# Recurrent stage of a two-block model: gated inputs on GpSimd, the third convolution one unit later

## The chip, the cores and the metric

The program runs on one core of a Trainium2 chip. The metric is the device time of one execution in microseconds (us). The core has TensorE (PE in the profile; its weight loads are PEld), VectorE (DVE), ScalarE (ACT), GpSimd (POOL) and SyncE (SP), each with an instruction queue of its own that is worked off in order. They meet through semaphores.

## The reference, cut to what matters

The reference is two blocks of two layers each on 512 tokens of width 1024, in float32. The change touches only the recurrent mixer, which runs once, in the last layer of the second block:

```python
proj = h @ w_in                                   # 1024 -> 2048
gate, xr = jnp.split(proj, 2, axis=-1)
gate = jax.nn.gelu(gate, approximate=True)
xc = conv(xr, conv_w) + conv_b                    # causal, 4 taps, one filter per channel
r = sigmoid(einsum('bsni,nij->bsnj', xg, w_a) + b_a)   # xg is xc in 4 blocks of 256 channels
i = sigmoid(einsum('bsni,nij->bsnj', xg, w_i) + b_i)
log_a = -8 * r * softplus(-lam)
a = exp(log_a)
u = sqrt(-expm1(2 * log_a)) * (i * xc)
hs[t] = a[t] * hs[t-1] + u[t]                     # an associative scan over time
return (hs * gate) @ w_out
```

The product that changes its engine is `i * xc`.

## The kernel before

Activations lie transposed: 128 channels on the partitions, the 512 tokens along the free dimension, so a 1024-wide tensor is 8 blocks [128, 512]. A float32 matmul is made of three: weights and activations are split into a high and a low part, and hi·hi, lo·hi and hi·lo are summed in PSUM.

The input projection of the recurrent stage is 16 **units** (u0 to u15), each 8 chunks of three matmuls. Units 0 to 7 give the blocks of `xr` (tile rgx), 8 to 15 those of `gate` (rggate). For each unit the raw weights come by DMA into `wraw`, ScalarE rounds them to `whi` (L238), VectorE subtracts to get `wlo` (L245), and only then may TensorE begin the unit: it waits for `w_split`. `whi` and `wlo` have two slots. VectorE also takes every finished unit out of PSUM (L1026).

The rest of the mixer runs beside these units. Every engine walks one common list, `order`: position 8u+c stands for chunk c of unit u, and the table `beside` (L3056 to L3073) names what is to be issued behind that chunk. The steps are:

- conv (pair p, L2979): the convolution of blocks 2p and 2p+1 on VectorE, two scalings (L2982) and six multiply-adds (L2988), then the semaphore rg_xc. It stands at 19, 35, 51 and 67.
- gates (block b, L2993 and L3005): four float32 matmul instructions on TensorE (L3001, two for each of the two gates; the trace shows each as two), then on ScalarE two sigmoids into rgA and rgU (L3007, L3008) and a tanh into rgTH (L3010), which raises rg_gates. At 29, 33, 45, 49, 76, 81, 86, 91.
- input (block b, L3012): VectorE multiplies rgU by rgxc (L3014), two positions behind its gates.
- logs (block b, L3016 and L3025): ScalarE takes two logarithms and an exponential (L3020, L3021, L3023), VectorE subtracts (L3027). At 53, 57, 61, 65 for blocks 0 to 3 and at 94, 98, 102, 106 for the others.
- mult (block b, L3029 and L3033): ScalarE's last exponential (L3031), then VectorE's product rgU by rgTH (L3035) and the scan over time (L3037), two positions behind the logs.
- gelu, gated and mix close the stage. GpSimd does six of the eight gated products (L3046), its only work in this stage next to two weight DMAs.

In each unit the rounding of the next unit's weights stands at chunk 1 on ScalarE, the low part at chunk 2 on VectorE, and the previous unit's evacuation at chunk 0. So at one position VectorE meets the unit's own work first and then the entries of `beside`.

```python
if kk == 0 and u:
    evac(u - 1)
if kk == 2 and u >= 2:
    lo_part(v, 0, st, u + 1, body[u + 1] if u + 1 < nu else st["next"])
```

Of the kernel before, what the change touches and what calls it, by code (L numbers as in the profile page):

```python
# [9 lines left out]
ALU = mybir.AluOpType  # L10
# [87 lines left out]
def build_program(nc, t, out):  # L98

    with ExitStack() as ctx:  # L100
# [58 lines left out]
        def S(name):  # L159
            if name not in sems:  # L160
                sems[name] = ctx.enter_context(nc.semaphore(name))
            return sems[name]
# [2279 lines left out]
        for l in range(DEPTH):  # L2442
            full = l < DEPTH - 1
            n = TOK if full else SEQ
            v = lambda kind, l=l: (lambda b, s: scl[:, 3 * l + kind, 2 * b + s:2 * b + s + 1])
# [458 lines left out]
        def recurrent(m, last, gpost):  # L2904
# [6 lines left out]
            xr, A, U, xc, gate, TH = (here_at(n_, j) for j, n_ in enumerate(("rgx", "rgA", "rgU", "rgxc", "rggate", "rgTH")))  # L2911
            mlo, mhi = here_at("mix3lo", 0, F32R), here_at("mix3hi", 1, F32R)
            xcr, gm, p1, lns, lnd, mul, hs, gel, gp, mh, ml = (S(f"rg_{n_}") for n_ in (
                "xc", "mm", "gates", "logs", "logdiff", "mult", "hs", "gelu", "gated", "mixhi", "mixlo"))
            col = lambda name, i: VC[:, 2, B2ROW[name] + i:B2ROW[name] + i + 1]

            body, outs = [], []
# [47 lines left out]
            def dve_units(v):  # L2965
                def evac(u):
                    v.wait_ge(S("w_used"), g0 + u + 1)
                    outs[u][1](v, 0, u, unit_bank(u)).then_inc(S(f"evac_done{u % 2}"), 1)
                for u in range(nu):
                    for kk in range(8):  # L2970
# [4 lines that stand above are left out]
                        yield  # L2975
                evac(nu - 1)
                yield

            def dve_conv(v, pair):  # L2979
                for b in (2 * pair, 2 * pair + 1):  # L2980
                    v.wait_ge(*evacuated(b))
                    v.tensor_scalar(xc[:, b, :], xr[:, b, :], col("rg_conv_w", 24 + b), col("rg_conv_b", b),  # L2982
                                    ALU.mult, ALU.add)
                for j in range(3):
                    v.drain()
                    sh = 3 - j
                    for b in (2 * pair, 2 * pair + 1):
                        v.scalar_tensor_tensor(out=xc[:, b, sh:SEQ], in0=xr[:, b, 0:SEQ - sh],  # L2988
                                               scalar=col("rg_conv_w", 8 * j + b), in1=xc[:, b, sh:SEQ],
                                               op0=ALU.mult, op1=ALU.add)  # L2990
                v.drain().then_inc(xcr, 1)
# [17 lines left out]
                a.drain()  # L3009
                a.activation(TH[:, b, :], A[:, b, :], ACT.Tanh, scale=scl[:, 6, b:b + 1]).then_inc(p1, 1)  # L3010

            def dve_input(v, b):  # L3012
                v.wait_ge(p1, b + 1)
                v.tensor_tensor(U[:, b, :], U[:, b, :], xc[:, b, :], ALU.mult)  # L3014

            def act_logs(a, b):  # L3016
                if b % 4 == 0:
# [7 lines left out]
            def dve_logs(v, b):  # L3025
                v.wait_ge(lns, b + 1)
                v.tensor_tensor(TH[:, b, :], xr[:, b, :], TH[:, b, :], ALU.subtract).then_inc(lnd, 1)  # L3027
# [3 lines left out]
                a.activation(TH[:, b, :], TH[:, b, :], ACT.Exp, scale=0.5).then_inc(mul, 1)  # L3031

            def dve_scan(v, b):  # L3033
                v.wait_ge(mul, b + 1)
                v.tensor_tensor(U[:, b, :], U[:, b, :], TH[:, b, :], ALU.mult)  # L3035
                v.drain()
                v.tensor_tensor_scan(TH[:, b, :], A[:, b, :], U[:, b, :], 0.0, ALU.mult, ALU.add).then_inc(hs, 1)  # L3037
# [5 lines left out]
            def gated(e, b):  # L3043
                e.wait_ge(gel, b + 1)
                e.wait_ge(hs, b + 1)
                e.tensor_tensor(TH[:, b, :], TH[:, b, :], gate[:, b, :], ALU.mult).then_inc(gp, 1)  # L3046
# [5 lines left out]
            def dve_mixlo(v, b):  # L3052
                v.wait_ge(mh, b + 1)
                v.tensor_tensor(mlo[:, b, :], TH[:, b, :], mhi[:, b, :].bitcast(F32), ALU.subtract).then_inc(ml, 1)
# [2 lines left out]

            def put(at, *names):
                beside.setdefault(at, []).extend(names)
            for pair in range(4):  # L3060
                put(16 * pair + 19, ("conv", pair))
            for b, at in enumerate((29, 33, 45, 49, 76, 81, 86, 91)):
                put(at, ("gates", b))
                put(at + 2, ("input", b))
            for first, at in ((0, 53), (4, 94)):
                for j in range(4):
                    put(at + 4 * j, ("logs", first + j))
# [39 lines left out]
            def dve_program(v):  # L3107
                ramp.dve(v, st)
                dense = dve_units(v)
                for name, b in order:  # L3110
                    if name == "unit":
                        next(dense, None)
                    elif name == "conv":
                        dve_conv(v, b)
                    elif name == "input":
                        dve_input(v, b)
                    elif name == "logs":
                        dve_logs(v, b)
                    elif name == "mult":
                        dve_scan(v, b)  # L3120
                    elif name == "gated":
                        v.wait_ge(gp, b)
                        gated(v, b)
                    elif name == "mix":
                        dve_mixlo(v, b)

            def pool_program(pool):
                pool.wait_ge(S("phase_end"), 3 * phase_of["rg"])
                pool.dma_start(wa[:], t["rg_w_a_2"][0].rearrange("n (k p) j -> p (n k) j", p=P)).then_inc(S("rg_w"), 16)
                pool.dma_start(wi[:], t["rg_w_i_2"][0].rearrange("n (k p) j -> p (n k) j", p=P)).then_inc(S("rg_w"), 16)  # L3130
                for b in range(6):
                    gated(pool, b)
            phase_of["rg"] = len(phases)
            return mhi, mlo, dict(pool=pool_program, sp=lambda sp: sp_stage(sp, st), pe=pe_program, act=act_program,
                                  dve=dve_program), lambda k: (ml, k + 1)


# [5 lines left out]
        m, last = ffn(0, m0, last, b2("mix_post"))  # L3143

        *mixed, rg_part, rg_ready = recurrent(m, last, b2("ffn_post"))
        m1 = arena("mo1", [P, NB, SEQ], off=24 * K1)
        st, last, zero = squares_beside("b21", m1, in_arena, lambda ev: plain("wout3", t["rg_w_out_2"][0], 0, 8, SEQ,
# [116 lines left out]
```

## Time and profile before

| | |
|---|---|
| median of 3 runs | 2548.02 us (2547.56 to 2548.71) |
| the profiled execution's own time | 2550.76 us |
| its span | 2548.9 us |
| TensorE busy in the span | 94% |
| mean granted TensorE clock | 0.986 |
| recurrent units (u0 to u15) | about 1966.9 to 2098.9 us of the span |

TensorE is busy nearly all the time; a change elsewhere moves the end only where TensorE waits. In the timeline rows a number in brackets is the idle time of that engine just ahead of the row and what ended it. A matmul row's duration (0.39 us) is a pipelined one: matmuls start 0.23 us apart.

### The profile page before, as it was taken

The page shows a single profiled execution, that of the slowest core. Times are in us where ns is not written, and L with a number is a line of the kernel's source. Part 1 is how long each engine was busy: PE and PEld are TensorE (multiplying, and loading weights), DVE is VectorE, ACT ScalarE, POOL GpSimd, SP SyncE. Part 2 cuts the span into 40 slices and gives each one's busy share as a digit, 9 for nine tenths or more (in the row PEclk, how much of TensorE's full clock was granted, in tenths as well). Part 3 has the DMA queues.
Part 4 walks back from the last instruction along what each step waited for, and adds up shares of the span by engine and source line. Part 5 has one row for each costly group of instructions (what it writes and reads, how often), then busy time and mean ns, then how long its engine had stood idle before and what let it go on. Part 6 is the DMA issues. An engine that isn't in the chain of part 4 may idle for free.

```text
span 2548.9 us, 48743 instructions
## 1 busy us (share of the span) xinstructions
PE 2389.9 (94%) x20392; PEld 1885.1 (74%) x20392; DVE 1339.7 (53%) x2135; ACT 999.5 (39%) x1675; POOL 160.6 (6%) x213
## 2 busy tenths in 40 slices
PE   7999999888989999888899998999999999999999
PEld 5777777777767766787676666788887667788887
DVE  4347644556464654555567763655523664555422
ACT  3225443444343445354445554322223554322222
POOL 0000000343000000144000000000000010000000
PEclk9999999999999999999999999999999999999999
DMA  7721111000102111100131212233333222233332
GB/s 272 253 80 34 34 46 50 19 5 12 50 25 83 42 42 55 50 4 4 51 99 58 58 50 67 74 99 99 97 91 118 58 66 75 83 96 93 99 95 79
DMA packets 300551, 182.65 MB, mean 72 GB/s; under 512 B 5290, under 2 KB 284476, under 8 KB 300236
## 3 DMA queue, kind: packets, MB, share of 16 engines
q1 hardware_dynamic: 286940, 150.50, 20.2%
q10 hardware_dynamic: 12480, 25.17, 2.8%
q0 software_dynamic: 944, 4.27, 0.5%
q8 instruction: 144, 2.36, 0.4%
q14 instruction: 43, 0.35, 0.0%
HBM read 177.80 MB, written 2.12 MB: 71 GB/s over the span
## 4 chain that ended last, share of the span: by engine, by line
PE 80%; DVE 9%; ACT 5%; issue 3%; DVEq 3%; ACTq 1%; DMA 0%; SPq 0%
PE PW L323 11%; PE PW L325 11%; PE PW L324 11%; PE PW L413 6%; PE PW L414 6%; PE PW L415 6%; PE PW L1224 2%; PE PW L1267 2%; PE PW L1810 2%; PE PW L1805 1%; PE PW L1793 1%; DVE wlo L245 1%; PE PW L3001 1%; PE PW L980 1%; PE PW L598 1%
## 5 line engine op out<-in xcount | busy, mean ns | idle before, releaser
L245 DVE TENSOR_TENSOR wlo<-wraw,whi 128x1024 fp32r<-128x1024 f32 (+1 forms) x272 | 329.5, 1212 | 376.1 <-ACT whi L238 355.1
L238 ACT ACTIVATE whi<-wraw 128x1024 fp32r<-128x1024 f32 (+1 forms) x272 | 283.6, 1043 | 267.5 <-PE PW L325 256.4
L413 PE MATMUL PW<-hhi,whi 128*128 128x512 f32 (+1 forms) x880 | 323.7, 368 | 11.7 <-DVEq L3210 7.0
L323 PE MATMUL PW<-hhi,whi 128*128 128x512 f32 (+1 forms) x824 | 315.4, 383 | 0.0
L324 PE MATMUL PW<-hhi,wlo 128*128 128x512 f32 (+1 forms) x824 | 315.0, 382 | 0.0
L325 PE MATMUL PW<-hlo,whi 128*128 128x512 f32 (+1 forms) x824 | 314.9, 382 | 0.0
L414 PE MATMUL PW<-hhi,wlo 128*128 128x512 f32 (+1 forms) x880 | 306.1, 348 | 0.0
L415 PE MATMUL PW<-hlo,whi 128*128 128x512 f32 (+1 forms) x880 | 305.8, 348 | 0.0
L413 PEld LDWEIGHTS PW<-hhi,whi 128*128 128x128 f32 x880 | 167.6, 190 | 57.5 <-issue 24.0
L414 PEld LDWEIGHTS PW<-hhi,wlo 128*128 128x128 f32 x880 | 167.9, 191 | 21.8 <-issue 3.3
L415 PEld LDWEIGHTS PW<-hlo,whi 128*128 128x128 f32 x880 | 167.5, 190 | 21.7
L323 PEld LDWEIGHTS PW<-hhi,whi 128*128 128x128 f32 x824 | 155.2, 188 | 30.6 <-DVE wlo L245 0.7
L324 PEld LDWEIGHTS PW<-hhi,wlo 128*128 128x128 f32 x824 | 155.2, 188 | 30.2
L325 PEld LDWEIGHTS PW<-hlo,whi 128*128 128x128 f32 x824 | 155.1, 188 | 30.0
L323 PE MATMUL PW<-fhi,whi 128*128 128x512 f32 x352 | 138.7, 394 | 0.0
L325 PE MATMUL PW<-flo,whi 128*128 128x512 f32 x352 | 138.0, 392 | 0.0
L324 PE MATMUL PW<-fhi,wlo 128*128 128x512 f32 x352 | 136.6, 388 | 0.0
L1026 DVE TENSOR_TENSOR gb<-PW,xT 128x512 f32<-128x512 f32 x88 | 60.7, 692 | 115.3 <-PE PW L325 110.8
L1997 ACT ACTIVATE XX<-PW 128x512 f32<-128x512 f32 (+1 forms) x120 | 66.5, 554 | 118.2 <-PE PW L1810 115.3
L2860 ACT ACTIVATE gb<-gb 128x512 f32<-128x512 f32 x44 | 27.8, 632 | 210.7 <-DVE gb L1026 210.7
L1810 PE MATMUL PW<-XX,Tt 64*64 64x64 f32 x1920 | 101.6, 223 | 3.5 <-issue 2.8
L1805 PE MATMUL PW<-Tt,XX 64*64 64x64 f32 x1536 | 81.3, 233 | 16.9 <-DVE Tt L2082 12.7
(477 smaller groups left out, 4425.6 us busy)
## 6 DMA issues: line engine op xcount, KB each, us to landing
wraw<-in_w_in SPq DMA_DIRECT2D x68, 512.0 KB, 3.8
mod_w<-in_mod_w ACTq DMA_DIRECT2D x12, 2048.0 KB, 10.8
wraw<-in_ffn_w_gate SPq DMA_DIRECT2D x44, 512.0 KB, 3.8
wraw<-in_ffn_w_up SPq DMA_DIRECT2D x44, 512.0 KB, 3.8
wraw<-in_ffn_w_down SPq DMA_DIRECT2D x32, 512.0 KB, 3.8
wraw<-in_attn_w_in SPq DMA_DIRECT2D x24, 512.0 KB, 3.8
wraw<-in_w_out SPq DMA_DIRECT2D x16, 512.0 KB, 3.8
wraw<-in_rg_w_in SPq DMA_DIRECT2D x16, 512.0 KB, 4.0
```

Source lines behind the costliest of these rows:

```text
L238: act.activation(whi[:, slot, 0:kb, :], wraw[:, slot, 0:kb, :], ACT.Copy).then_inc(S("w_hi"), 1)
L245: dve.tensor_tensor(wlo[:, slot, 0:kb, :], wraw[:, slot, 0:kb, :], whi[:, slot, 0:kb, :].bitcast(F32), ALU.subtract).then_inc(S("w_split"), 1)
L323: pe.matmul(acc, wh[:, k, :], rhi[:, k0 + k, s0:s1], start=a, stop=False)
L324: pe.matmul(acc, wl[:, k, :], rhi[:, k0 + k, s0:s1], start=False, stop=False)
L325: last_mm = pe.matmul(acc, wh[:, k, :], rlo[:, k0 + k, s0:s1], start=False, stop=b)
L413: e.matmul(acc, whi[:, u % 2, k, :], rhi[:, k0 + k, s0:s1], start=k == 0, stop=False)
L414: e.matmul(acc, wlo[:, u % 2, k, :], rhi[:, k0 + k, s0:s1], start=False, stop=False)
L415: ins = e.matmul(acc, whi[:, u % 2, k, :], rlo[:, k0 + k, s0:s1], start=False, stop=k == kb - 1)
L1026: return v.tensor_tensor(self.halves(dest), self.halves(acc), self.rstd, ALU.mult)
L1805: return e.matmul(at(384 + 128 * e_ + CH * hp)[half(pi), :], XX[tp, i, 0, :], Tt[tp, i, :], start=True, stop=True)
L1810: return e.matmul(at(128 * e_ + CH * hp)[tp, :], Tt[tp, i, :], XX[tp, i, 0, :], start=True, stop=True)
L1997: a.activation(dst, src, ACT.Copy).then_inc(X_out.sem, 1)
```

## The change

GpSimd computes `i * xc` instead of VectorE, all eight blocks in a row, each when its rg_gates comes. A new semaphore, rg_entered, is raised by each product, and VectorE waits for it ahead of the product in the mult step. The convolution of pair 2 moves from position 51 (unit 6) to 59 (unit 7); the other pairs stay.

```diff
+            entered = Signal("rg_entered", 8)
...
-            def dve_input(v, b):
-                v.wait_ge(p1, b + 1)
-                v.tensor_tensor(U[:, b, :], U[:, b, :], xc[:, b, :], ALU.mult)
+            def pool_input(g, b):
+                g.wait_ge(p1, b + 1)
+                g.tensor_tensor(U[:, b, :], U[:, b, :], xc[:, b, :], ALU.mult).then_inc(entered.sem, 1)
...
             def dve_scan(v, b):
+                v.wait_ge(entered.sem, entered.at(b + 1))
                 v.wait_ge(mul, b + 1)
...
-            for pair in range(4):
-                put(16 * pair + 19, ("conv", pair))
+            for at, pair in zip((19, 35, 59, 67), range(4)):
+                put(at, ("conv", pair))
...
-                put(at + 2, ("input", b))
...
-                    elif name == "input":
-                        dve_input(v, b)
...
+                for b in range(8):
+                    pool_input(pool, b)
                 for b in range(6):
                     gated(pool, b)
```

VectorE's row before, from the low part of unit 7 to the scan of block 1. L2982 and L2988 are a convolution, L3014 an input, L3027 the logs' difference, L3035 and L3037 the product and the scan of the mult step.

```order
L245 TENSOR_TENSOR wlo<-wraw,whi 128x1024
L2982 TENSOR_SCALAR rgxc<-rgx,VC 128x512 x2
L2988 SCALAR_TENSOR_TENSOR rgxc<-rgx,VC,rgxc 128x509 x2
...
L3014 TENSOR_TENSOR rgU<-rgU,rgxc 128x512
L3027 TENSOR_TENSOR rgTH<-rgx,rgTH 128x512
L3035 TENSOR_TENSOR rgU<-rgU,rgTH 128x512
L3037 SCALAR_TENSOR_TENSOR rgTH<-rgA,rgU 128x512
L1026 TENSOR_TENSOR rgx<-PW,xT 128x512
L3027 TENSOR_TENSOR rgTH<-rgx,rgTH 128x512
L245 TENSOR_TENSOR wlo<-wraw,whi 128x1024
L3035 TENSOR_TENSOR rgU<-rgU,rgTH 128x512
L3037 SCALAR_TENSOR_TENSOR rgTH<-rgA,rgU 128x512
```

The same place now, where the lines are L3028 for the difference, L3037 and L3039 for product and scan, and L2983 and L2989 for the convolution:

```order
L245 TENSOR_TENSOR wlo<-wraw,whi 128x1024
L3028 TENSOR_TENSOR rgTH<-rgx,rgTH 128x512
L3037 TENSOR_TENSOR rgU<-rgU,rgTH 128x512
L3039 SCALAR_TENSOR_TENSOR rgTH<-rgA,rgU 128x512
L1026 TENSOR_TENSOR rgx<-PW,xT 128x512
L3028 TENSOR_TENSOR rgTH<-rgx,rgTH 128x512
L245 TENSOR_TENSOR wlo<-wraw,whi 128x1024
L2983 TENSOR_SCALAR rgxc<-rgx,VC 128x512 x2
L2989 SCALAR_TENSOR_TENSOR rgxc<-rgx,VC,rgxc 128x509 x2
...
L3037 TENSOR_TENSOR rgU<-rgU,rgTH 128x512
L3039 SCALAR_TENSOR_TENSOR rgTH<-rgA,rgU 128x512
L3028 TENSOR_TENSOR rgTH<-rgx,rgTH 128x512
```

The convolution of pair 2 has moved from ahead of the first difference to between the low part of unit 8 and the mult step of block 1; the input of block 3 is gone from the row. GpSimd's row in this stage, as a difference:

```order
-L3129 DMA rgwa<-in_rg_w_a 128x8x256
-L3130 DMA rgwi<-in_rg_w_i 128x8x256
-L3046 TENSOR_TENSOR rgTH<-rgTH,rggate 128x512 x6
+L3128 DMA rgwa<-in_rg_w_a 128x8x256
+L3129 DMA rgwi<-in_rg_w_i 128x8x256
+L3015 TENSOR_TENSOR rgU<-rgU,rgxc 128x512 x8
+L3048 TENSOR_TENSOR rgTH<-rgTH,rggate 128x512 x6
```

The eight products stand behind the weight DMAs and ahead of the gated products.

## Rows read from the trace of the kernel before

**Rows 1.** The page, first lines: busy us (share of the span) xinstructions
```profile
span 2548.9 us, 48743 instructions
PE 2389.9 (94%) x20392; PEld 1885.1 (74%) x20392; DVE 1339.7 (53%) x2135; ACT 999.5 (39%) x1675; POOL 160.6 (6%) x213
```

**Rows 2.** TensorE's waits, 1985 to 2110 us: us in total, times, longest
```profile
PE PW L2951 <- DVE wlo L245: 6.5, 4, 2.1
```

**Rows 3.** Timeline, first work of u8, u9, u10: start, us, [idle before <-releaser]
```profile
2033.87 0.50 PE L2951 MATMUL PW<-h3hi,whi 128*128 128x512 f32 x1 [2.10 <-DVE wlo L245]
...
2041.75 0.19 PEld L2951 LDWEIGHTS PW<-h3hi,whi 128*128 128x128 f32 x1 [0.96 <-DVE wlo L245]
...
2050.95 0.19 PEld L2951 LDWEIGHTS PW<-h3hi,whi 128*128 128x128 f32 x1 [0.44 <-DVE wlo L245]
```

**Rows 4.** Timeline of VectorE, from the convolution of pair 2
```profile
2020.54 1.00 DVE L2982 TENSOR_SCALAR rgxc<-rgx,VC 128x512 f32<-128x512 f32 x2
...
2026.11 0.69 DVE L3014 TENSOR_TENSOR rgU<-rgU,rgxc 128x512 f32<-128x512 f32 x1
2027.72 0.69 DVE L3027 TENSOR_TENSOR rgTH<-rgx,rgTH 128x512 f32<-128x512 f32 x1 [0.91 <-ACT rgTH L3023]
...
2031.98 0.69 DVE L3027 TENSOR_TENSOR rgTH<-rgx,rgTH 128x512 f32<-128x512 f32 x1 [0.30 <-ACT rgTH L3023]
2032.59 1.22 DVE L245 TENSOR_TENSOR wlo<-wraw,whi 128x1024 fp32r<-128x1024 f32 x1
2033.73 0.69 DVE L3035 TENSOR_TENSOR rgU<-rgU,rgTH 128x512 f32<-128x512 f32 x1
...
2035.63 0.67 DVE L3027 TENSOR_TENSOR rgTH<-rgx,rgTH 128x512 f32<-128x512 f32 x1
...
2040.48 1.22 DVE L245 TENSOR_TENSOR wlo<-wraw,whi 128x1024 fp32r<-128x1024 f32 x1
```

**Rows 5.** Timeline of ScalarE: table load behind block 3's gates; behind the difference
```profile
2024.35 1.28 ACT L3018 ACT_TABLE_LOAD   x1
...
2036.33 0.63 ACT L3031 ACTIVATE rgTH<-rgTH 128x512 f32<-128x512 f32 x1 [1.06 <-DVE rgTH L3027]
2036.87 1.04 ACT L238 ACTIVATE whi<-wraw 128x1024 fp32r<-128x1024 f32 x1
```

**Rows 6.** The chain that ended last, in order of time: start, us, what
```profile
2034.49 1.22 DVE rgTH L3037
2035.71 0.59 DVE rgTH L3027
```

**Rows 7.** By stretch: busy PE, PEld, DVE, ACT, POOL; PEclk, DMA share, GB/s
```profile
2026.20:2051.00 24.80, 22.15 (x82) 15.84 (x80) 21.15 (x27) 15.76 (x23) 0.00 (x0) 0.93 0.15 43
...
2034.70:2038.10 3.40, 3.40 (x10) 2.64 (x9) 2.63 (x4) 2.34 (x4) 0.00 (x0) 0.51 0.54 154
...
1512.40:1519.30 6.90, 5.94 (x22) 3.89 (x22) 4.75 (x11) 4.95 (x11) 0.00 (x0) 0.51 0.06 11
...
2087.40:2090.40 3.00, 2.91 (x13) 2.40 (x14) 2.23 (x4) 2.31 (x3) 0.00 (x0) 1.00 0.56 170
```

**Rows 8.** Timeline of TensorE, two other long waits
```profile
1512.35 1.22 PE L2572 MATMUL PW<-k,q 64*128 64x256 f32 x4 [3.34 <-DVEq L2723]
2087.49 0.50 PE L2951 MATMUL PW<-h3hi,whi 128*128 128x512 f32 x1 [1.95 <-DVE wlo L245]
```

**Rows 9.** Waits, 1970 to 2135 us: the inputs' (us, times, longest)
```profile
DVE rgU L3014 <- ACT rgTH L3010: 22.8, 5, 7.2
```

**Rows 10.** Instructions by line: x count, ns min/median/max, first to last start us
```profile
L3014 DVE TENSOR_TENSOR rgU<-rgU,rgxc x8: 692/693/694, 2000.4 to 2071.9; 128x512 f32<-128x512 f32 x8
L3035 DVE TENSOR_TENSOR rgU<-rgU,rgTH x8: 686/692/696, 2029.1 to 2088.7; 128x512 f32<-128x512 f32 x8
...
L3046 POOL TENSOR_TENSOR rgTH<-rgTH,rggate x6: 1299/1724/2282, 2091.7 to 2100.0; 128x512 f32<-128x512 f32 x6
```

**Rows 11.** Timeline: convolution 1, the gates that read it, input 5
```profile
2003.84 4.39 DVE L2988 SCALAR_TENSOR_TENSOR rgxc<-rgx,VC,rgxc 128x509 f32<-128x509 f32 x6
...
2012.47 1.88 PE L3001 MATMUL PW<-rgxc,rgwa 128*128 128x512 f32 x4
...
2058.17 0.69 DVE L3014 TENSOR_TENSOR rgU<-rgU,rgxc 128x512 f32<-128x512 f32 x1 [4.73 <-ACT rgTH L3010]
```

## The prediction

> **What bounds the kernel now.** I read the page first [rows 1]: TensorE is busy for 94% of the span, so the end moves only with TensorE's work or its waits. GpSimd is busy for 6% and VectorE for 53%. The change leaves TensorE's instructions as they are, so the question is only what happens to its waits in the recurrent units. The view of waits gives them [rows 2]: 6.5 us in four waits, all for the low part of a unit's weights (wlo, L245) from VectorE. TensorE's timeline says where: 2.10 us ahead of u8 and a short one ahead of u9 [rows 3], and two just under 2 us ahead of u13 and u14, of which the last is in [rows 8]. (Seen from the weight loads, which run a little ahead, the wait of u9 is 0.96 us and u10 has one of 0.44.) Nowhere in these units does it wait for a convolution or a gate. So I ask of each moved instruction: does it stand ahead of one of these low parts on VectorE, with nothing idle in between?
>
> The timelines of VectorE and ScalarE [rows 4, 5] and the chain that ended last [rows 6] answer. Ahead of u8 the low part starts at 2032.59, right behind a difference (L3027) that waited for ScalarE; the difference before it, at 2027.72, had waited 0.91 us for ScalarE. ScalarE in turn came straight from the gates of block 3 on TensorE through a table load at 2024.35 and three activations. So the 2.10 us wait ahead of u8 is ScalarE's chain, not VectorE's load. Behind that low part it is the other way round: from 2033.73 VectorE goes without a pause through product, scan and the difference of block 2 (2035.63), and ScalarE waits 1.06 us for that difference, until 2036.33. Only then does it round the weights of u9 (2036.87), and the low part of u9 follows at 2040.48 by the same ping-pong. The scan and the difference are both links of the chain that ended last [rows 6].
>
> **The change part by part.**
>
> *Convolution of pair 2, taken from position 51.* It runs from 2020.54 to the next start at 2026.11 [rows 4], which is 5.57 us with its drains. Behind it come the input of block 3 and then 0.91 us of idle VectorE waiting for ScalarE. Taking it away makes that idle time longer and lets nothing start earlier: 0.
>
> *The same convolution, put at position 59.* There it stands between the low part of u8 and the product and scan of block 1. The low part of u8 is ahead of it, so u8 starts as before, at 2033.87. The convolution then takes 2033.73 to 2039.30, and everything behind it on VectorE moves by 5.57: product and scan of block 1, and the difference of block 2 from 2035.63 to 41.20. Is there slack on the way to u9? VectorE had none (the rows touch), ScalarE was already waiting for that difference, and from there to the low part each engine waits for the other or works. So the rounding of u9 goes from 2036.87 to 42.44, its low part from 2040.48 to 46.05, and u9 starts at 2041.75 + 5.57 = 2047.32. Its loads were through at 2041.75 − 0.96 = 2040.79 [rows 3], so the wait ahead of u9 grows from 0.96 to 6.5 us. The cost is **+5.57 us**.
>
> Does a later wait give it back? Convolution 3, the mult step of block 3, the evacuation of u8 and the low part of u10 follow in the old order, so u10's low part moves by the same 5.57. From u10 on, gates, ScalarE's chain and the waits ahead of u13 and u14 all start from TensorE's own gate matmuls and shift with them. 0 back.
>
> *TensorE's clock behind the longer wait.* After the 2.10 us wait the granted clock was 0.51 for 3.4 us [rows 3, 7], which is the 1.2 GHz level; after the 3.34 us wait at 1512.35 it was 0.51 for 6.9 us [rows 7, 8]; after the 1.95 us wait it stayed at 1.00 [rows 7, 8]. A wait of 6.5 us is beyond all of these, so I expect the low level behind it. At half speed 3.4 us cost 1.7 us of work and 6.9 us cost 3.45. The least would be 0. I take 1.7: the nearest row is the other wait on a low part in this same stage, and it had the short stretch. A part is absorbed: u10 is held by its low part for 0.44 us [rows 3], and TensorE may lose that much for free. Net 1.7 − 0.44, **+1.3 us**, ends 0 and +3.0. The low stretch at 2034.70 stays as it is, since the wait ahead of u8 stays; u9 waits for VectorE anyway.
>
> *Eight inputs taken from VectorE.* Each is 0.69 us [rows 10], 5.5 in all. Five of the eight end a wait of VectorE for ScalarE, 22.8 us in sum, the longest 7.2 ahead of input 2 [rows 9]: there VectorE has time to give away. Of the other three, input 1 has that 7.2 us wait behind it, input 3 the 0.91 us, input 4 the 4.73 us ahead of input 5 [rows 4, 11]. Gain 0; the upper bound, if every one counted, is 5.5.
>
> *Eight products on GpSimd.* The nearest rows are GpSimd's own products of the same shape: 1.30 us at the least, 1.72 at the median, 2.28 at the most [rows 10]. Nothing else is in its queue until the gated products at 2091.7. The new wait stands on VectorE ahead of the mult step, with the scan, an evacuation and a next low part queued behind it. Product and first use lie far apart: block 0's may start when input 0 did, at 2000.4, and is wanted at 2029.1; block 7's at 2071.9, wanted at 2088.7 [rows 10]; block 3's at about 2024.3, ahead of ScalarE's table load, wanted behind convolution 3. Cost 0, and the cover is gone only if a product took some 16 us.
>
> The two engines do disturb each other: beside VectorE's work the same GpSimd product took from 1.30 to 2.28 us [rows 10]. The Trainium skill ("SBUF — State Buffer", Who interferes with whom) says that a VectorE instruction with two SBUF inputs contends with a GpSimd instruction that reads SBUF, and that the later one is blocked for the other's whole length. By that rule product 1 could hold up convolution 1 by one product. The convolution ends at 2003.84 + 4.39 = 2008.2 and its gates start at 2012.47 [rows 11], so the sum is the same with the rule and without; a worse place is weighed as rival C.
>
> **The sum.** 5.57 + 1.3 = +6.9 us. The profiled execution has 2550.76, 2.7 above the median; against its own time this is 2557.6, against the median 2548.0 + 6.9 = **2554.9 us**, 0.27% slower. A measurement of this kernel can tell about 0.2% (5.1 us) from no change.
>
> **The rivals.**
>
> *A, not slower: the moved convolution falls into VectorE's waits.* In the 24.8 us around it VectorE is idle for 24.80 − 21.15 = 3.65 us [rows 7], and the 0.69 us of input 3 is gone. If all of that could be filled, 5.57 − 3.65 − 0.69 = 1.2 us would be left: 2549.2. It decides for itself from the point where the idle time lies between the low part of u8 and the one of u9 and not ahead of a wait for ScalarE. Against it: the idle pieces are waits for ScalarE's answer to VectorE's own last result, so they move with it.
>
> *B, faster: VectorE's relief ends the wait ahead of u8.* If the first difference had in truth waited for the convolution and input 3, the 2.1 us wait and the 1.7 us of low clock behind it would go, and u9 be earlier by as much: A's 2549.2 − 3.8 = 2545.4. Against it stands the 0.91 us of idle time that ends with ScalarE [rows 4].
>
> *C, slower still: port contention on the path.* Each of the four products of the second half, or four gated ones, holds up a low part by one median product: 4 × 1.72 = 6.9 us, so 2561.8. It decides once a product starts within 1.7 us ahead of a late low part or of what leads to it. For it: the spread of GpSimd's product between 1.30 and 2.28 us [rows 10]. Against it: the products start at the end of a block's tanh, and the low parts on which TensorE waits come later, when GpSimd has nothing to do: the low part of u9 at 2040.48 lies 16 us behind the last product of the first half.
>
> *D, the change does not do what it says.* VectorE's and GpSimd's rows show both moves; that leaves nothing for this case.
>
> **How the numbers follow.** The forecast has 0.85, A 0.08, B 0.03, C 0.04. The forecast's own range goes from no loss by the clock, 2548.0 + 5.6 = 2553.6, to the long low stretch, 2548.0 + 5.6 + 3.0 = 2556.6, and another 1.7 if one of the waits ahead of u13 and u14, now at other moments, is also followed by the low level: 2558.3. With a little of A below I set 2551.5 to 2558.5. Slower by over 0.2%: most of the forecast and C, 0.86. Within 0.2%: A and the forecast's lowest edge, 0.10. Faster: 0.04.
>
> **What would show it.** Right: VectorE idle from about 2020.6 until 2027.7; the low part of u8 at its old time; the convolution of pair 2 right behind it; a wait of TensorE ahead of u9 of 6 to 6.5 us on wlo; a clock of 0.5 in the 3 to 7 us behind that wait; waits ahead of u13 and u14 of just under 2 us as before; the last unit's end 7 to 8.6 us later; VectorE never waiting for rgU from GpSimd. Wrong: a difference at L3028 earlier than 2027.7 (B), a wait ahead of u9 well under 6 us (A), a VectorE wait on GpSimd or a low part of 2 us ahead of a TensorE wait (C).

## The result, and the profile after

The changed kernel takes 2555.98 us (median of 7 runs, 2553.15 to 2559.14) against 2548.02 before (7 runs, 2539.84 to 2553.56). The ratio is 1.0035, with a 95% interval of 1.0024 to 1.0045: 0.35% slower (the two medians alone are 0.31% apart). The forecast was 2554.9 us, slower.

The page's first lines, which answer to [rows 1]:

```profile
span 2553.7 us, 48751 instructions
## 1 busy us (share of the span) xinstructions
PE 2390.1 (94%) x20392; PEld 1885.7 (74%) x20392; DVE 1331.0 (52%) x2127; ACT 999.3 (39%) x1675; POOL 171.8 (7%) x221
```

TensorE's work is the same to 0.2 us, VectorE has 8 instructions fewer, GpSimd 8 more. TensorE's waits from 1985 to 2110 us (in total, times, longest), which answer to [rows 2]:

```profile
PE PW L2952 <- DVE wlo L245: 12.6, 4, 6.5
```

The four waits have doubled, and one of them is 6.5 us long. TensorE's timeline shows which, to be read beside [rows 3]; here the stage began 3.2 us earlier in the span than in the trace of before, so only distances compare:

```profile
2030.66 0.50 PE L2952 MATMUL PW<-h3hi,whi 128*128 128x512 f32 x1 [2.10 <-DVE wlo L245]
...
2044.58 0.80 PE L2952 MATMUL PW<-h3hi,whi 128*128 128x512 f32 x1 [6.52 <-DVE wlo L245]
...
2084.45 0.50 PE L2952 MATMUL PW<-h3hi,whi 128*128 128x512 f32 x1 [1.93 <-DVE wlo L245]
...
2092.27 0.50 PE L2952 MATMUL PW<-h3hi,whi 128*128 128x512 f32 x1 [2.08 <-DVE wlo L245]
```

u8 waits for 2.10 us as before, u9 for 6.52 instead of 0.54. u13 and u14 wait 1.93 and 2.08 us, where it was 1.86 and 1.95. VectorE's timeline from the first difference to the low part of u9, to be read beside [rows 4]:

```profile
2024.51 0.69 DVE L3028 TENSOR_TENSOR rgTH<-rgx,rgTH 128x512 f32<-128x512 f32 x1 [7.11 <-ACT rgTH L3024]
...
2029.39 1.22 DVE L245 TENSOR_TENSOR wlo<-wraw,whi 128x1024 fp32r<-128x1024 f32 x1
2030.52 1.00 DVE L2983 TENSOR_SCALAR rgxc<-rgx,VC 128x512 f32<-128x512 f32 x2
...
2034.96 1.41 DVE L2989 SCALAR_TENSOR_TENSOR rgxc<-rgx,VC,rgxc 128x511 f32<-128x511 f32 x2 [0.46 <-issue]
2036.56 0.69 DVE L3037 TENSOR_TENSOR rgU<-rgU,rgTH 128x512 f32<-128x512 f32 x1 [0.19 <-issue]
...
2038.47 0.67 DVE L3028 TENSOR_TENSOR rgTH<-rgx,rgTH 128x512 f32<-128x512 f32 x1
...
2043.31 1.22 DVE L245 TENSOR_TENSOR wlo<-wraw,whi 128x1024 fp32r<-128x1024 f32 x1
```

VectorE waits 7.11 us for ScalarE where the convolution used to be, and does the convolution where ScalarE waits for VectorE. ScalarE's row beside [rows 5]:

```profile
2039.17 0.63 ACT L3032 ACTIVATE rgTH<-rgTH 128x512 f32<-128x512 f32 x1 [7.11 <-DVE rgTH L3028]
```

That wait was 1.06 us. The clock behind u9's wait, by stretch as in [rows 7] (PEclk is the third value from the right):

```profile
2044.50:2048.70 4.20, 4.12 (x10) 3.25 (x11) 3.98 (x8) 1.78 (x2) 0.00 (x0) 0.50 0.43 125
2048.90:2055.00 6.10, 6.10 (x20) 3.64 (x20) 4.63 (x6) 1.16 (x2) 0.00 (x0) 0.99 0.01 3
```

For 4.2 us of u9's work TensorE ran at the 1.2 GHz level, and then at full speed.

There is a second new stretch at the low level, behind u14's wait. In [rows 7] the clock behind that wait was 1.00; here it is

```profile
2093.60:2096.50 2.90, 2.90 (x8) 2.28 (x7) 2.83 (x4) 2.87 (x4) 0.05 (x1) 0.50 0.54 161
```

### The profile page after: what moved, and what is told of

It is laid out like the page before. It is cut to its first block, busy times and chain, and to the rows that moved or that the text cites. A ratio compares the mean times of both kernels' runs of the same rounds, so it can differ in the third digit from the quotient of the medians.

```text
span 2553.7 us, 48751 instructions
## 1 busy us (share of the span) xinstructions
PE 2390.1 (94%) x20392; PEld 1885.7 (74%) x20392; DVE 1331.0 (52%) x2127; ACT 999.3 (39%) x1675; POOL 171.8 (7%) x221
## 4 chain that ended last, share of the span: by engine, by line
PE 79%; DVE 9%; ACT 5%; DVEq 3%; issue 3%; ACTq 1%; DMA 0%; SPq 0%
PE PW L323 11%; PE PW L325 11%; PE PW L324 11%; PE PW L413 6%; PE PW L414 6%; PE PW L415 6%; PE PW L1224 2%; PE PW L1267 2%; PE PW L1810 2%; PE PW L1805 1%; PE PW L1793 1%; DVE wlo L245 1%; PE PW L3002 1%; PE PW L598 1%; PE PW L980 1%
```

## The experiments

Each ran beside the kernel before. Whole runs scatter by some 5 us to either side, so two measures stand side by side: the ratio, and the **stage length** in the trace, from the first matmul of u2 (1984.99 us in the trace before) to the first wait of the output projection for a low part (2110.92 there). The stage length leaves out most of the scatter: u2 begins anywhere from 1979.6 to 1989.2 us in the twelve traces, while from the end of the stage to the end of the span it is 437.6 to 438.0 us in all of them, and from u2 to u8 48.87 or 48.88 us in the seven that have the old order there (before, changed, e1 to e4, e7).

| kernel | ratio to before (95%) | stage length, us | u8 to u9, us |
|---|---|---|---|
| before | | 125.9 | 7.88 |
| changed kernel | 1.0035 (1.0024 to 1.0045) | 134.0 | 13.92 |
| e1_products_only | 1.0001 (0.9991 to 1.0012) | 126.3 | 7.90 |
| e2_conv_only | 1.0035 (1.0023 to 1.0047) | 133.7 | 13.85 |
| e3_one_tap | 1.0005 (0.9994 to 1.0015) | 130.6 | 10.95 |
| e4_spin_ahead_of_u9 | 1.0020 (1.0010 to 1.0029) | 132.3 | 13.92 |
| e5_order_both | 0.9968 (0.9956 to 0.9980) | 119.5 | no wait |
| e6_order_first_half | 0.9974 (0.9965 to 0.9983) | 121.0 | no wait |
| e7_order_second_half | 1.0004 (0.9995 to 1.0013) | 124.8 | 7.89 |
| e8_order_both_dve_inputs | 0.9969 (0.9954 to 0.9983) | 119.5 | no wait |
| e9_gelu_split | 0.9966 (0.9952 to 0.9979) | 117.6 | no wait |
| e10_gated_on_dve | 0.9960 (0.9946 to 0.9975) | 117.5 | no wait |

**The two halves of the change apart.** Theory: all of the cost is the convolution's place. Rival: the products on GpSimd cost something themselves.

e1_products_only, against the changed kernel:

```diff
-            for at, pair in zip((19, 35, 59, 67), range(4)):
+            for at, pair in zip((19, 35, 51, 67), range(4)):
```

> The changed kernel with the convolution of pair 2 back at position 51; GpSimd's products stay. Position theory (the whole cost is the convolution's place): waits of TensorE ahead of u8, u9, u13, u14 as in the kernel before (2.1, 0.5, 1.9, 1.9 us), first gated start of u9 7.9 us behind that of u8, time 2548 (2546 to 2550), ratio to before 1.000. Rival (the products on GpSimd cost something themselves, by blocking VectorE or by the new wait): at least one of these waits longer by 1 us or more, time 2550 or above. In both, convolution 1 takes about 0.9 us longer beside product 1, as in the changed kernel.

e2_conv_only, against the kernel before:

```diff
-            for pair in range(4):
-                put(16 * pair + 19, ("conv", pair))
+            for at, pair in zip((19, 35, 59, 67), range(4)):
+                put(at, ("conv", pair))
```

> The kernel before with the convolution of pair 2 at position 59; the products stay on VectorE. Position theory: u9 starts 13.9 us behind u8 instead of 7.9, wait ahead of u9 6.5 us, low clock behind it, time 2555.5 (2553.5 to 2557.5), ratio 1.003. Rival (the cost needs the products on GpSimd too, or the products on VectorE would add to it): wait ahead of u9 differs from 6.5 us by over 0.5, or the time stays under 2552 or goes over 2558.

The products alone give 2548.92 us, 1.0001, and this row of TensorE's waits up to 2090 us:

```profile
PE PW L2952 <- DVE wlo L245: 6.6, 4, 2.1
```

The convolution alone gives 1.0035, the ratio of the whole change, and TensorE's row for u9 is

```profile
2043.60 0.79 PE L2951 MATMUL PW<-h3hi,whi 128*128 128x512 f32 x1 [6.50 <-DVE wlo L245]
```

So the move of the convolution is the whole measurable cost. The products add 0.4 us to the stage (126.3 against 125.9, and 134.0 against 133.7). The likely source is the added wait for rg_entered ahead of the product of the mult step. Behind a convolution that place shows 0.19 us of issue in the changed kernel's VectorE row above and in e1, and none in the kernel before and in e2. With it u13 and u14 wait 0.07 and 0.13 us longer. The median of e2 (2558.28) is above the bound of 2558 that was set for the rival; the ratio and the 6.50 us wait say that this is the scatter of the runs.

**The length of what is moved.** e3_one_tap, against the changed kernel:

```diff
-                for j in range(3):
+                for j in range(1 if pair == 2 else 3):
```

> The changed kernel with only the first of the three multiply-add rounds of the convolution of pair 2 (two taps of four are left out for blocks 4 and 5), so that the moved piece lasts about 2.5 us instead of 5.6. Position theory: the wait ahead of u9 follows the length of what was moved: 0.5 + 2.5 = 3.0 to 3.5 us instead of 6.5, time 2551 to 2553. Rival (a fixed price of the place, for instance a missed slot or the clock alone): wait of about 6.5 or about 0.5 us.

```profile
2044.29 0.50 PE L2952 MATMUL PW<-h3hi,whi 128*128 128x512 f32 x1 [3.58 <-DVE wlo L245]
```

The wait is 3.58 us, between 0.5 and 6.5: it follows the length of the moved piece (2.67 us here) and is no fixed price of the place. The stage is 4.6 us longer than before: 3.1 us between u8 and u9, 1.3 behind u9, where the granted clock was 0.58 for 3.9 us, and 0.2 further on. The whole run came out at 2551.4, inside what was expected, but its ratio of 1.0005 stands for 1.3 us, less than the stage shows; that gap is about the width of the interval (up to 1.0015, 3.8 us) and was not followed up.

**The clock.** e4_spin_ahead_of_u9, against the changed kernel:

```diff
                         if kk == 0:
+                            if u == 9:
+                                spin(e, 7, 26)
                             e.wait_ge(S("w_split"), g0 + u + 1)
```

> The changed kernel, with 26 small matmuls into a free PSUM bank ahead of u9, which fill the 6.5 us wait and are added work. Clock theory (of the 8 us, 6 are the wait and 2 the low clock behind it, less 0.4 absorbed): u9 starts as late as before, but at the full clock, and u10 starts 9.2 us behind u9 instead of 11.3; time 2554 (2552 to 2555.5), 2 us under the changed kernel. Rival (the 2 us ahead of u10 are VectorE's longer row, not the clock): u10 still 11.3 us behind u9, time 2556.

The stretches of the wait and of u9's work in this kernel:

```profile
2036.00:2042.30 6.30, 5.63 (x51) 5.43 (x49) 5.23 (x8) 4.53 (x7) 0.00 (x0) 1.00 0.00 0
2042.30:2048.00 5.70, 5.64 (x20) 3.87 (x21) 5.29 (x10) 1.77 (x2) 0.00 (x0) 1.00 0.31 92
```

The small matmuls (128x128) and the end of u8 fill 5.6 of 6.3 us, the clock stays at full speed, and u10 follows u9 by 9.27 us, as in the kernel before (9.20) and not as in the changed kernel (11.12). u9 itself starts as late as in the changed kernel, 13.92 us behind u8. The stage is 1.7 us shorter than the changed kernel's. So the low clock is a cost of its own, 1.7 us of the 8.1; 6.0 are the wait, and 0.4 what e1 shows for the products. The ratios alone would not show it: the intervals of e4 and of the changed kernel overlap.

**Using what was learned.** If VectorE and ScalarE work between the end of a unit and the next low part is what costs, turning the order must gain: next unit's rounding and low part first, mult step and next logs behind. e5_order_both, against the changed kernel:

```diff
-            for at, pair in zip((19, 35, 59, 67), range(4)):
+            for at, pair in zip((19, 35, 51, 75), range(4)):
...
-            for first, at in ((0, 53), (4, 94)):
-                for j in range(4):
-                    put(at + 4 * j, ("logs", first + j))
-                    put(at + 4 * j + 2, ("mult", first + j))
+            for b, (at, after) in enumerate(((53, 58), (59, 66), (67, 69), (70, 74), (94, 98), (99, 106), (107, 109), (110, 114))):
+                put(at, ("logs", b))
+                put(after, ("mult", b))
```

> Products on GpSimd, convolution 2 back at 51, convolution 3 at 75, behind the low part of u10; and in both halves the order is turned at each unit: the next unit's rounding and low part stand ahead of a block's mult step and of the next logs (logs at 53, 59, 67, 70, 94, 99, 107, 110; mult at 58, 66, 69, 74, 98, 106, 109, 114). Position theory (what costs is VectorE and ScalarE work between the end of a unit and the next unit's low part): the waits ahead of u8, u9, u10, u13 and u14 (2.5, 1.0, 0.4, 2.3 and 2.4 us by the weight loads in the kernel before) go to under 1 us in sum, and the low clock behind u8 with them: u8 to u14 shorter by 8 to 10 us, time 2539 to 2542. Rival (the same chain of ScalarE work must fit somewhere and the wait only moves, to the gates or to the end of the stage): time 2546 to 2550.

All of TensorE's waits for a low part in the units of this kernel, by its loads, and the longest wait of the next stage's first rows:

```profile
2071.02 0.19 PEld L2952 LDWEIGHTS PW<-h3hi,whi 128*128 128x128 f32 x1 [0.21 <-DVE wlo L245]
...
2082.78 0.19 PEld L2952 LDWEIGHTS PW<-h3hi,whi 128*128 128x128 f32 x1 [1.02 <-DVE wlo L245]
...
2091.12 0.47 PE L323 MATMUL PW<-mix3hi,whi 128*128 128x512 f32 x1 [2.60 <-DVE mix3lo L3056]
```

u8, u9, u10 and u14 no longer wait, u13 waits 0.21 us. Up to u14 the gain of 8 to 10 us that was expected is there: u14 starts 93.1 us behind u2 instead of 102.5. But the stage is only 6.4 us shorter and the time 0.32% less (2543.8 us, where 2539 to 2542 were expected). The missing 3 us are lost at the other two rows: a new 1.02 us ahead of u15, and 2.60 us in the next stage for the first products of the gate. Behind that wait the granted clock is low for some 10 us, against 3.4 us in the next stage's first rows before, and yet from the first matmul of the next stage to the end of the stage it is 11.9 us in both kernels:

```profile
2091.50:2101.50 10.00, 8.84 (x20) 5.39 (x19) 8.44 (x11) 5.61 (x8) 2.29 (x2) 0.50 0.12 35
```

So theory and rival were both partly right, and two runs say where.

e6_order_first_half, against e5 (the second half at its old order):

```diff
-... (94, 98), (99, 106), (107, 109), (110, 114))):
+... (94, 96), (98, 100), (102, 104), (106, 108))):
```

> As e5_order_both, but only blocks 0 to 3 (logs at 53, 59, 67, 70, mult at 58, 66, 69, 74; convolution 3 at 75); blocks 4 to 7 as in the kernel before. Position theory: no wait ahead of u8, u9 and u10, u13 and u14 wait as before; u8 to u10 from 17.1 to 14.4 us and u8 itself 2.5 us earlier; time 2543 to 2545. Rival: 2547 to 2550, with a new wait ahead of the gates of block 4 or 6.

e7_order_second_half, against e5 (the first half and convolution 3 as before):

```diff
-            for at, pair in zip((19, 35, 51, 75), range(4)):
+            for at, pair in zip((19, 35, 51, 67), range(4)):
...
-            for b, (at, after) in enumerate(((53, 58), (59, 66), (67, 69), (70, 74), ...
+            for b, (at, after) in enumerate(((53, 55), (57, 59), (61, 63), (65, 67), ...
```

> As e5_order_both, but only blocks 4 to 7 (logs at 94, 99, 107, 110, mult at 98, 106, 109, 114); the first half as in the kernel before, with the products on GpSimd. Position theory: waits ahead of u13 and u14 under 0.5 us each, time 2544 to 2546. Rival: the gelus and mixes at the end wait instead, time 2547 to 2550.

e6 takes the first four pairs and the convolutions of e5's tables (blocks 4 to 7 at their old places) and brings 4.9 us of the 6.4; u14's wait fell with it, to 0.45 us, which was not expected. e7 takes the last four (logs and mult of blocks 0 to 3 and convolution 3 at their old places) and brings 1.1, with a ratio of 1.0004, as its rival had it; its waits ahead of u13 and u14 are gone as in e5, and the 1.02 us ahead of u15 and 2.60 us for a low part of the mix appear behind. In the first half a removed wait is a gain, and in the second half it moves to the end of the stage, where ScalarE's gelus and GpSimd's gated products come due.

e8_order_both_dve_inputs is e5 with the products back on VectorE; against the kernel before only the order differs:

```diff
-            for pair in range(4):
-                put(16 * pair + 19, ("conv", pair))
+            for at, pair in zip((19, 35, 51, 75), range(4)):
+                put(at, ("conv", pair))
...
-            for first, at in ((0, 53), (4, 94)):
-                for j in range(4):
-                    put(at + 4 * j, ("logs", first + j))
-                    put(at + 4 * j + 2, ("mult", first + j))
+            for b, (at, after) in enumerate(((53, 58), (59, 66), (67, 69), (70, 74), (94, 98), (99, 106), (107, 109), (110, 114))):
+                put(at, ("logs", b))
+                put(after, ("mult", b))
```

> The order of e5_order_both with the eight products on VectorE, as in the kernel before. If the products' engine matters nowhere, also where VectorE's row is tighter: same waits and time as e5_order_both within 1 us. Rival (GpSimd's help pays once the waits are gone): a wait of 0.5 us or more comes back at one of the units, time 1 to 4 us above e5_order_both.

Its stage is as long as that of e5, 119.5 us, and the ratio the same. GpSimd's help with `i * xc` is worth nothing in either order.

**The end of the stage.** e9_gelu_split, against e5:

```diff
-            put(119, *[("gelu", b) for b in range(6)])
-            put(122, ("gelu", 6))
-            for b in range(3):
-                put(122 + b, ("mix", b))
+            put(119, *[("gelu", b) for b in range(3)])
+            put(122, ("mix", 0), ("gelu", 3), ("mix", 1), ("gelu", 4), ("mix", 2), ("gelu", 5), ("gelu", 6))
```

> e5_order_both with the end of the stage re-ordered: only three gelus ahead of the rounding of the next stage's weights (position 119), the other four and the first three mixes at 122, alternating. In e5 TensorE waits 2.6 us ahead of the second chunk row of the next stage, behind a 2.04 us wait of VectorE for that rounding. If that queueing on ScalarE is what holds the end, this wait shrinks below 1 us, time 1 to 3 us under e5_order_both (about 2541 where before is 2549 to 2551, ratio 0.9958). Rival (the gated products on GpSimd, 10 us for six, set the end): the wait moves to the later mixes and the time stays within 1 us of e5_order_both (ratio 0.9968).

e10_gated_on_dve puts the six gated products on VectorE as well, two of them ahead of mix 0, the others one by one between the mixes. The first of them has no earlier gated product to wait for. Against e9:

```diff
-            put(122, ("mix", 0), ("gelu", 3), ("mix", 1), ("gelu", 4), ("mix", 2), ("gelu", 5), ("gelu", 6))
+            put(122, ("gated", 0), ("gated", 1), ("mix", 0), ("gelu", 3), ("gated", 2), ("mix", 1), ("gelu", 4), ("mix", 2),
+                ("gelu", 5), ("gelu", 6))
...
-            order += [("unit", nu), ("gelu", 7), ("mix", 3), ("gated", 6), ("mix", 4), ("gated", 7), ("mix", 5), ("mix", 6), ("mix", 7)]
+            order += [("unit", nu), ("gelu", 7), ("gated", 3), ("gated", 4), ("mix", 3), ("gated", 5), ("mix", 4), ("gated", 6), ("mix", 5),
+                      ("gated", 7), ("mix", 6), ("mix", 7)]
...
-                for b in range(6):
-                    gated(pool, b)
```

> e9_gelu_split with the six gated products of GpSimd on VectorE too, so that GpSimd does only the eight input products. Contention theory (where VectorE waits for the shared port on the path, GpSimd's help costs what it saves): the low part of the next stage back to 1.22 us from 2.06, the mixes to 0.69 each from 1.7, six products of 0.69 added to VectorE; end of the stage within 1 us of e9_gelu_split. Rival (GpSimd really relieves VectorE here): 2 to 4 us slower than e9_gelu_split.

In e9 the 2.60 us shrink to 0.21, and 1.97 us come up three blocks later:

```profile
2093.36 0.47 PE L323 MATMUL PW<-mix3hi,whi 128*128 128x512 f32 x1 [0.21 <-DVE mix3lo L3056]
...
2099.59 0.71 PE L323 MATMUL PW<-mix3hi,whi 128*128 128x512 f32 x1 [1.97 <-DVE mix3lo L3056]
```

So the wait shrank as the theory had it and also moved to a later mix as the rival had it. The stage is 1.9 us shorter than in e5; the ratio, 0.9966 against 0.9968, can't tell them apart. e10 has the same stage length without any gated product on GpSimd (117.5 against 117.6). The two kernels' mixes on VectorE, e9 first, then the first of e10:

```profile
2091.43 5.17 DVE L3056 TENSOR_TENSOR mix3lo<-rgTH,mix3hi 128x512 fp32r<-128x512 f32 x3
```
```profile
2094.00 0.69 DVE L3056 TENSOR_TENSOR mix3lo<-rgTH,mix3hi 128x512 fp32r<-128x512 f32 x1
```

1.72 us each beside GpSimd, 0.69 without it. Six products of 0.69 more on VectorE cost no more than running beside GpSimd did. e10 has the lowest ratio of this study, 0.9960 of before (0.9946 to 0.9975), some 10 us, of which 8.4 show in the stage; e5, e9 and e10 lie within each other's intervals.

## Why the prediction was right, point by point

- **Which wait.** The convolution had idle time behind it at its old place, and none on the way from its new one to the low part of u9. Both held: the first difference still starts on ScalarE's word (7.11 us idle instead of 0.91), and the low part of u8 is as late as ever (2.10 us wait). e1 and e2 show the two halves apart.
- **Its size.** +5.57 us was said for u8 to u9; it was 13.92 − 7.88 = 6.04. The forecast took the duration at the old place, 5.57 us from the convolution's start to the next instruction of VectorE. At the new one it was 5.97 us in e2 and 6.04 in the changed kernel. 0.07 of that go with the added semaphore wait, which e2 does not have. The other 0.40 come with an idle piece of 0.46 us that the profile puts to issue. It ends 2.8 to 4.3 us behind u8's start in e2, e3, e4 and the changed kernel, in e3 behind the convolution, and the kernel before and e1 do not have it. Its cause is open. The forecast wait of 6.5 us was reckoned by the weight loads (0.96 + 5.57); by the loads it was 6.95 us, and that the matmul's row shows 6.52 is no confirmation of the 5.57.
- **The clock.** +1.3 us was said, of 1.7 lost less 0.44 absorbed. The low level was there for 4.2 us of work, which is about 2.1 lost. The gates of block 5, in u10, start 12.48 us behind u9 instead of 10.69, so 1.8 were left and only 0.3 absorbed; e4 takes 1.7 away. The range of 0 to 3.0 held; 4.2 us lie between the two stretches of [rows 7], and the choice of the shorter one cost 0.4 us.
- **The inputs, taken off VectorE.** 0 was said, with an upper bound of 5.5; e1's stage is 0.4 us longer, not shorter, and e8 shows the same with the waits gone.
- **The products on GpSimd.** 0 was said. Each took 1.28 to 1.29 us, less than the 1.30 to 2.28 of the gated ones, and no VectorE instruction waited for the result of one. The overlooked part is, as far as the rows show it, the second semaphore wait itself, 0.07 to 0.13 us wherever the mult step leads to a late low part.
- **Nothing given back.** u13 and u14 wait as before, and the stage ends 8.1 us later. The sum by steps is 6.04 + 1.8 + 0.3 = 8.1 us, against 6.9 forecast and 8.0 between the medians.
- **One sign was missed.** The last unit was to end 7 to 8.6 us later; its last matmul starts 9.6 us later (122.92 us behind u2 instead of 113.30). The cause is the low level behind u14, for which the upper edge of the range had allowed 1.7 us: u15 follows u14 by 7.21 us instead of 5.59. It did not reach the end. Before, TensorE waited 0.35 and 0.66 us for the low parts of the first mixes in the next stage; now both waits are gone, because it comes there later. From u14 to the end of the stage it is 23.4 to 23.6 us in all six kernels of that order, in the four with the low level behind u14 (changed, e1, e2, e3) and in the two without (before, e4).
- **The rivals.** A and B fell with the first point. C has its mechanism but not its place: product 1 did hold up convolution 1 (below), which was still done 3.3 us ahead of the gates that read it. At the end of the stage the same does lie on the path, in the kernel before too: there the first three mixes took 5.14 us together, and TensorE waited for the low parts of mixes five times, 3.5 us in all. e10 takes this away and pays with six products on VectorE.

## What to carry to other kernels

A step that moves costs its own length where the two engines behind it are waiting for each other, and gains nothing at a place that had idle time behind it; the row to look for is a wait of the other engine that ends with the very instruction ahead of which the step is put. Where a unit's operand must be ready for the matrix engine, issue its preparation first and the rest behind it: that alone was worth 0.3% here, while giving VectorE's work to GpSimd was worth nothing. A long wait can cost more than its length: behind the one of 6.5 us the granted clock was at its lower level for 4.2 us of work, which added 1.7 us, and behind the one of u8, 2.1 us long in both kernels, it was so for about 3.4 us [rows 7]. The length of the wait alone does not tell: ahead of u14 it was 2.08 us in e1, with the low level behind it, and 2.09 us in e4, without. And a low clock costs time only where TensorE has no later wait to make it up from; behind u14 it cost nothing.

## What the runs showed of the hardware

Of a GpSimd product and a VectorE instruction with two inputs that meet, the one that starts second is held up. The multiply-adds of the four convolutions, before and after (x count, ns min/median/max):

```profile
L2988 DVE SCALAR_TENSOR_TENSOR rgxc<-rgx,VC,rgxc x24: 741/748/752, 1988.6 to 2046.3; 128x509 f32<-128x509 f32 x8, 128x510 f32<-128x510 f32 x8, 128x511 f32<-128x511 f32 x8
```
```profile
L2989 DVE SCALAR_TENSOR_TENSOR rgxc<-rgx,VC,rgxc x24: 740/748/1670, 1985.4 to 2049.1; 128x509 f32<-128x509 f32 x8, 128x510 f32<-128x510 f32 x8, 128x511 f32<-128x511 f32 x8
```

The slow one and the product that ran beside it in the changed kernel:

```profile
2003.43 1.29 POOL L3015 TENSOR_TENSOR rgU<-rgU,rgxc 128x512 f32<-128x512 f32 x1 [4.87 <-ACT rgTH L3011]
```
```profile
2003.60 2.33 DVE L2989 SCALAR_TENSOR_TENSOR rgxc<-rgx,VC,rgxc 128x511 f32<-128x511 f32 x2
```

The product ran from 2003.43 to 2004.72. The multiply-add that began at 2003.60 took 1.67 us, its neighbours 0.75: it was held up by 0.92 us of the 1.12 us that the product still had to run. VectorE's low parts, which meet the product in the same way, took 1.47 and 1.46 us instead of 1.22 in units 4 and 6; the product had 0.39 and 0.38 us left to run, and they lost 0.25 and 0.24. The Trainium skill ("SBUF — State Buffer", Who interferes with whom) has a VectorE instruction with two SBUF inputs contend with a GpSimd instruction that reads SBUF, calls the port pair that they share an exclusive lock, and says that issue order decides who blocks. The trace agrees in kind: the second one loses the overlap less 0.14 to 0.20 us.

It works the other way round too. In the kernel before, a gated product began inside a low part that had itself begun beside the product ahead of it:

```profile
2095.19 2.00 DVE L245 TENSOR_TENSOR wlo<-wraw,whi 128x1024 fp32r<-128x1024 f32 x1 [1.22 <-ACT whi L238]
```
```profile
2096.05 2.28 POOL L3046 TENSOR_TENSOR rgTH<-rgTH,rggate 128x512 f32<-128x512 f32 x1
```

It took 2.28 us, 0.98 more than the shortest of its kind (1.30), and the low part had 1.14 us left to run.

Filling a wait with small matmuls that nobody reads kept the clock up and gave 1.7 us of stage length back (e4), a patch for a wait that can't be removed.
